# A transformer block and a routed block: the first projection's pages move to the normed input, the last nineteen of them in high and low halves

## The chip, the core and the metric

The kernel runs on one core of one Trainium2 chip. The metric is the device time of one execution in microseconds (us). Five engines take part: TensorE (PE in the rows, its weight loads PEld), VectorE (DVE), ScalarE (ACT), GpSimd (POOL), and SyncE (SP), which only issues DMAs here.

## What is computed

The reference is a mixing block on 256 tokens of width 1024, a feed-forward block, and a second block with product-key experts. What matters here is its beginning:

```python
h = rms_norm(x, norm1_g[l])
proj = h @ w_in[l]
p_rwkv, p_sb, q_mem, gate_logits = jnp.split(proj, cut, axis=-1)

def rms_norm(x, g, eps=NORM_EPS):
    xf = x.astype(jnp.float32)
    y = xf * lax.rsqrt(jnp.mean(xf * xf, axis=-1, keepdims=True) + eps)
    return (y * g.astype(jnp.float32)).astype(x.dtype)

def token_shift(p, mu):
    prev = jnp.pad(p, ((0, 0), (1, 0), (0, 0)))[:, :-1]
    return p + (prev - p) * mu
```

The first 1792 columns of `proj` (14 tiles of 128) go through `token_shift` and then into a recurrence whose triangular systems the kernel solves by repeated squaring on blocks of 32, 64 and 128 tokens. The next 12 tiles are the queries and keys of the stick-breaking attention and the queries of the memory attention.

## The kernel before

Features lie on the 128 partitions, tokens on the free axis. A weight page is 128 x 1024 float32 (512 KB): the weights of one output tile of 128 features, read as eight 128 x 128 blocks. SyncE streams all pages in one order through a ring of four slots; a slot is loaded again once TensorE has counted its page in `page_done`. Four PSUM banks (0 to 3) take the output tiles of the pages in turn, so tile n waits until tile n-4 is out of its bank (`bank_free`, by the table `OWNER`). Banks 4 to 7 serve the small products in between.

Stage `in_a` has 26 pages, numbered 0 to 25. `a_page` multiplies page by page in float32, eight matmuls of 256 columns each, with `xg`, the input times its gain but not yet divided by its root mean square; that division is made on the way out. `evict(b, shift)` on VectorE waits for page b, multiplies the bank by the reciprocal root (L1634) and, for the first 14 pages, makes the token shift with three more operations (L1638 to L1640). `A_ORDER` gives the tile of each page: two tiles of low-rank inputs, the keys, the receptances, the values, then the 12 tiles without shift.

Between the pages stand the small products of the recurrence, written out by hand in one order for each engine, with counting semaphores: `b_pe`, `b_act` and `b_dve` carry named steps. The ones that matter here: `kk_sq` (squares of the keys, DVE L1684), `kk_sum` (their sums, PE L603, after page 8), the square root on ACT (L1146), the reciprocal on DVE (L1710, `kk_inv`), the spread of it on PE (L608, after page 11), the cumulated log decay on DVE (scans L1696 and L1703, L1713 and L1714, `cum_ready`), its exponentials on ACT (L1148 to L1150), the products with them on DVE up to `scaled` (L1741), and then the first near products on PE (L636), before and after page 18. Pages 19 to 25 alternate with products of 32 x 32 blocks (L516) and of pairs (L542). `pairs(j)` on PE waits until DVE has read `pairs(j-1)` (`pairs_read`).

The full normed input `hn` is made by `norm_apply(0, ...)` on DVE behind `evict(19)`. A later stage, `gate0` and `gate1`, already works in halves: `high(page)` on ACT rounds a page to float32r (L1101), `low(n)` on POOL subtracts this from the page (L2303), TensorE makes three one-pass products (high x high, high x low, low x high) in place of one float32 product, and the rounded input `hn_hi` and its rest `hn_lo_early` are made once (ACT L1173, DVE L1791). POOL does nothing else before that but two trees of three additions each (L2334), which sum the squares of the input and of the memory; the second one waits for `kk_sq`. `norm_apply(1, ...)`, the normed memory, follows `evict(23)`, and a memset of `DT` stands behind `kk_sq` (L1685).

## Time and profile before

| | |
|---|---|
| Median of 3 runs | 1410.83 us (1409.07 to 1412.17) |
| The profiled execution's own time | 1410.49 us |
| Its span in the trace | 1408.7 us |
| PE busy | 1277.8 us, 91% of the span |
| DVE, ACT, POOL busy | 835.1, 626.1, 583.8 us |
| Granted TensorE clock, mean | 0.993 of full |

A busy time says how long an engine had an instruction running, not that it was needed for the end; the profiled time is 1.8 us over the span, and 0.34 us under the median of the runs. The stage `in_a` fills the span from about 8.6 us to 133.7 us.

### The profile page before, as it was taken

The page shows a single profiled execution, that of the slowest core. Times are in us where ns is not written, and L with a number is a line of the kernel's source. Part 1 is how long each engine was busy: PE and PEld are TensorE (multiplying, and loading weights), DVE is VectorE, ACT ScalarE, POOL GpSimd, SP SyncE. Part 2 cuts the span into 40 slices and gives each one's busy share as a digit, 9 for nine tenths or more (in the row PEclk, how much of TensorE's full clock was granted, in tenths as well). Part 3 has the DMA queues.
Part 4 walks back from the last instruction along what each step waited for, and adds up shares of the span by engine and source line. Part 5 has one row for each costly group of instructions (what it writes and reads, how often), then busy time and mean ns, then how long its engine had stood idle before and what let it go on. Part 6 is the DMA issues. An engine that isn't in the chain of part 4 may idle for free.

```text
span 1408.7 us, 22241 instructions
## 1 busy us (share of the span) xinstructions
PE 1277.8 (91%) x8716; PEld 902.6 (64%) x8716; DVE 835.1 (59%) x1898; ACT 626.1 (44%) x1451; POOL 583.8 (41%) x390
## 2 busy tenths in 40 slices
PE   7999999999999999999999999999777778877786
PEld 6888897989999999987897544444222223222222
DVE  3865201454557873477347766667776666677754
ACT  4210232656566664553454544444443444444433
POOL 1100022515878889740043444444434443443341
PEclk9999999999999999999999999999999999999999
DMA  6332322324645555443369999999999999999995
GB/s 241 120 117 83 106 91 74 120 92 149 194 158 188 181 186 191 164 135 99 135 235 390 396 421 421 422 421 421 422 422 421 421 421 422 421 422 422 421 422 230
DMA packets 67652, 381.06 MB, mean 271 GB/s; under 512 B 7520, under 2 KB 7648, under 8 KB 34528
## 3 DMA queue, kind: packets, MB, share of 16 engines
q0 software_dynamic: 36864, 268.45, 46.0%
q1 hardware_dynamic: 29808, 107.49, 23.0%
q10 hardware_dynamic: 880, 3.76, 0.8%
q8 instruction: 65, 1.06, 0.3%
q14 instruction: 35, 0.29, 0.1%
HBM read 378.63 MB, written 1.05 MB: 270 GB/s over the span
## 4 chain that ended last, share of the span: by engine, by line
PE 61%; DMA 26%; DVE 5%; ACT 5%; issue 2%; POOL 1%; DVEq 0%; POOLq 0%; ACTq 0%
DMA arena_block<-in_experts,arena_block 26%; PE bank L429 25%; PE bank L1041 10%; PE bank L465 4%; PE bank L981 3%; PE bank L483 3%; DVE arena_block L2247 2%; PE bank L427 2%; PE bank L447 2%; PE bank L853 1%; PE bank L516 1%; ACT arena_block L1535 1%; PE bank L542 1%; ACT arena_block L1533 1%; POOL w_lo L2305 1%
## 5 line engine op out<-in xcount | busy, mean ns | idle before, releaser
L1041 PE MATMUL bank<-arena_block 128*128 128x512 f32 x1024 | 493.7, 617 | 101.6 <-ACT arena_block L1535 101.5
L1041 PEld LDWEIGHTS bank<-arena_block 128*128 128x128 f32 x1024 | 182.3, 192 | 400.9 <-ACT arena_block L1535 247.7
L2247 DVE SCALAR_TENSOR_TENSOR arena_block<-arena_block 128x1024 f32<-128x1024 f32 x256 | 313.5, 1226 | 196.8 <-DMA arena_block<-in_experts,arena_block 196.2
L2323 POOL DMA_INDIRECT arena_block<-in_experts,arena_block x256 | 271.6, 1061 | 378.8 <-PE bank L1041 349.9
L2305 POOL TENSOR_TENSOR w_lo<-ring,w_hi 128x1024 fp32r<-128x1024 f32 x108 | 262.2, 2447 | 184.4 <-ACT w_hi L1101 183.9
L1529 ACT ACTIVATE arena_block<-arena_block 128x1 f32<-128x1 f32 x256 | 51.8, 202 | 322.9 <-DVE arena_block L2247 322.6
L1101 ACT ACTIVATE w_hi<-ring 128x1024 fp32r<-128x1024 f32 x116 | 122.0, 1054 | 60.4 <-PE bank L465 28.8
L429 PE MATMUL bank<-x_hi,w_hi 128*128 128x256 f32 x384 | 109.3, 285 | 1.6 <-POOL w_lo L2305 1.5
L429 PE MATMUL bank<-arena_mix,ring 128*128 128x256 f32 x480 | 109.1, 384 | 0.0
L429 PE MATMUL bank<-x_lo,w_hi 128*128 128x256 f32 x384 | 108.7, 283 | 0.0
L429 PE MATMUL bank<-x_hi,w_lo 128*128 128x256 f32 x384 | 108.7, 283 | 0.0
L1535 ACT ACTIVATE arena_block<-const,arena_block 128x128 f32<-128x128 f32 x256 | 102.7, 401 | 8.3
L429 PEld LDWEIGHTS bank<-arena_mix,ring 128*128 128x128 f32 x480 | 90.4, 191 | 16.0 <-issue 4.1
L2303 POOL TENSOR_TENSOR ring_lo<-ring,early_hi 128x1024 fp32r<-128x1024 f32 x8 | 19.9, 2488 | 171.4 <-ACT early_hi L1101 171.4
L1533 ACT ACTIVATE arena_block<-arena_block 128x1 f32<-128x1 f32 x256 | 75.4, 295 | 9.3
L429 PEld LDWEIGHTS bank<-x_hi,w_hi 128*128 128x128 f32 x384 | 73.7, 192 | 2.0 <-POOL w_lo L2305 2.0
L429 PEld LDWEIGHTS bank<-x_lo,w_hi 128*128 128x128 f32 x384 | 73.7, 192 | 0.1
L429 PEld LDWEIGHTS bank<-x_hi,w_lo 128*128 128x128 f32 x384 | 73.7, 192 | 0.0
L429 PE MATMUL bank<-h_norm,ring 128*128 128x256 f32 x224 | 51.6, 383 | 0.0
L465 PE MATMUL bank<-ff_hi,w_hi 128*128 128x256 f32 x176 | 49.8, 283 | 0.0
L465 PE MATMUL bank<-ff_lo,w_hi 128*128 128x256 f32 x176 | 49.8, 283 | 0.0
L465 PE MATMUL bank<-ff_hi,w_lo 128*128 128x256 f32 x176 | 49.8, 283 | 0.0
(512 smaller groups left out, 2245.1 us busy)
## 6 DMA issues: line engine op xcount, KB each, us to landing
ring<-in_pages SPq DMA_DIRECT2D x189, 512.0 KB, 3.9
late<-in_pages SPq DMA_DIRECT2D x11, 512.0 KB, 6.0
arena_block<-in_experts,arena_block POOLq DMA_INDIRECT x256, 15.3
x_res<-in_xT SPq DMA_DIRECT2D x2, 512.0 KB, 6.0
arena_mix<-in_memT ACTq DMA_DIRECT2D x1, 1024.0 KB, 10.7
arena_block<-in_subkT ACTq DMA_DIRECT2D x1, 1024.0 KB, 4.9
out_tok<-arena_block SPq DMA_DIRECT2D x4, 256.0 KB, 4.7
const<-in_const ACTq DMA_DIRECT2D x1, 974.5 KB, 6.8
```

The costliest lines, as they stand in the source:

```text
L429: last = mm(out[:, 0:T], w, y, **flags)
L465: last = mm(out[:, 0:T], w[:, at * P:(at + 1) * P], y[:, k, :], start=k == 0 and n_ == 0, stop=k == FT - 1 and n_ == 2)
L483: last = mm(bank_of(stage, 2 * b + t)[:, 0:T], w[:, t * 512 + k * P:t * 512 + (k + 1) * P], y[:, k, :], start=k == 0 and n_ == 0, stop=k = ...
L981: last = mm(bank[4 + b % 2][:, 0:T], w[:, k * P:(k + 1) * P], hn[:, k, :], start=k == 0, stop=k == KT - 1)
L1041: last = mm(bank[2 * tt + j][:, :], diag[:, slot, :], uv[slot][:, D + j * 512:D + (j + 1) * 512], start=False, stop=stop)
L1101: A_(w, ring[:, page % SLOTS, :], ACT.Copy).then_inc(S("hi_ready"), 1)
L1529: A_(e_gelu[:, s:s + 1], e_act[:, s:s + 1], ACT.Gelu).then_inc(S("gelu_ready"), 1)
L1533: A_(e_act[:, s:s + 1], e_gelu[:, s:s + 1], ACT.Copy, scale=gate_p[:, tt, m:m + 1]).then_inc(S("weight_ready"), 1)
L1535: A_(diag[:, s, :], ident, ACT.Copy, scale=e_act[:, s:s + 1]).then_inc(S("diag_ready"), 1)
L2247: stt(uv[s][:, 0:D], uv[s][:, 0:D], 1.0, htok[:, tt, :], ALU.mult, ALU.mult, accum_out=e_act[:, s:s + 1])\
L2305: nc.gpsimd.tensor_tensor(w_lo[:, slot, :], ring[:, slot, :], w_hi[:, slot, :].bitcast(F32), ALU.subtract)\
L2323: nc.gpsimd.indirect_dma_start(out=uv[slot], out_offset=None, in_=A["experts"], in_offset=bass.IndirectOffsetOnAxis(ap=eidx[:, tt, m:m + 1 ...
```

## The change

Pages 0 to 4 stay as they are. Pages 5 and 6 are multiplied, still in float32, with `hn`, and pages 7 to 25 in high and low halves of page and input. For this `hn` is made right behind `evict(1)`; ACT rounds it (`hn_hi_first`), DVE makes the rest (`hn_lo_early`), ACT rounds the nineteen pages and POOL makes their low halves in place of the ring's slot. Since `hn` is divided by the root already, the outputs are not scaled any more. For pages 5 to 13 ACT writes (1 - mu) times the bank into `proj` (`a_part`) and DVE adds mu times the bank shifted by one token (`shift`). Pages 14 to 25 are copied out by ACT (`a_copy`); DVE has nothing to do with them. The second tree of POOL stands behind the second low half, the memset of `DT` and the normed memory behind `near_cross(3)`.

```diff
-SPLIT = EARLY + [p for p in range(SPLIT0, N_PAGES) if p not in WHOLE]
+SHIFTED, ROWED, FIRST_SPLIT = 14, 5, 7
+FIRSTS = list(range(PAGE0["in_a"] + FIRST_SPLIT, PAGE0["in_a"] + N_IN_A))
+IN_PLACE = FIRSTS + EARLY
+SPLIT = IN_PLACE + [p for p in range(SPLIT0, N_PAGES) if p not in WHOLE]
+OWNER[SHIFTED:N_IN_A] = [("in_a_copy", i) for i in range(N_IN_A - SHIFTED)]
...
         def a_page(first, n=1):
-            linear("in_a", xg, part=(first, n))
+            for b in range(first, first + n):
+                if b < ROWED:
+                    linear("in_a", xg, part=(b, 1))
+                    continue
+                if b == ROWED:
+                    pe.wait_ge(S("norm_out"), 1)
+                if b == FIRST_SPLIT:
+                    pe.wait_ge(S("hn_low_early"), 1)
+                if b < FIRST_SPLIT:
+                    linear("in_a", hn, part=(b, 1))
+                else:
+                    linear("in_a", hn_hi_first, hn_lo_early, part=(b, 1))
...
+        def a_part(b):
+            act.wait_ge(S("page_done"), PAGE0["in_a"] + b + 1)
+            i = A_ORDER[b]
+            A_(proj[:, i, :], bank_of("in_a", b)[:, 0:T], ACT.Identity, scale=mu_rest[:, i:i + 1]).then_inc(S("in_a_part"), 1)
+        def a_copy(b):
+            act.wait_ge(S("page_done"), PAGE0["in_a"] + b + 1)
+            A_(proj[:, A_ORDER[b], :], bank_of("in_a", b)[:, 0:T], ACT.Copy).then_inc(S("in_a_copy"), 1)
+        def a_high(b):
+            high(PAGE0["in_a"] + b)
...
+        act.wait_ge(S("norm_out"), 1)
+        A_(hn_hi_first, hn, ACT.Copy).then_inc(S("hn_first"), 1)
+        a_high(7)
...
         act.wait_ge(S("b_dve"), B_DVE["kk_mean"])
         A_(row[0:8, :], row[0:8, :], ACT.Sqrt).then_inc(S("b_act"), 1)
+        a_part(9)
+        a_high(12)
+        a_part(10)
         act.wait_ge(S("b_dve"), B_DVE["cum_ready"])
         A_(tmp1, cc, ACT.Exp).then_inc(S("b_act"), 1)
+        a_high(13)
+        a_part(11)
...
+        def shift(b):
+            i = A_ORDER[b]
+            dve.wait_ge(S("in_a_part"), b - ROWED + 1)
+            stt(proj[:, i, 1:T], bank_of("in_a", b)[:, 0:T - 1], V("mu", i), proj[:, i, 1:T], ALU.mult, ALU.add).then_inc(S("in_a_out"), 1)
...
-        evict(0, True)
-        evict(1, True).then_inc(S("b_dve"), 1)
-        for b in range(2, 6):
-            last = evict(b, True)
+        evict(0)
+        evict(1).then_inc(S("b_dve"), 1)
+        norm_apply(0, x, "norm1_g", hn)
+        for b in range(2, ROWED):
+            last = evict(b)
         step(last)
+        dve.wait_ge(S("page_done"), PAGE0["in_a"] + ROWED)
+        dve.wait_ge(S("hn_first"), 1)
+        tt_(hn_lo_early, hn, hn_hi_first.bitcast(F32), ALU.subtract).then_inc(S("hn_low_early"), 1)
+        shift(5)
...
         tt_(tmp2, kk, kk, ALU.mult).then_inc(S("b_dve"), 1)
-        v.memset(DT, 0.0)
         dve.wait_ge(S("b_act"), B_ACT["lora_taken"])
...
         near_cross(3)
+        dve.wait_ge(S("in_a_copy"), N_IN_A - SHIFTED)
+        v.memset(DT, 0.0)
+        norm_apply(1, mem_raw, "mem_g", memn)
         pairs_read(6)
...
-        for i in range(2):
+        def square_tree(i):
...
+        square_tree(0)
         for n in range(len(SPLIT)):
             low(n)
+            if n == 1:
+                square_tree(1)
```

On POOL, from the start of the program: arena_mix rows are the trees, ring_lo rows the low halves. Before, both trees stand ahead of the low halves, the first of which belongs to a gate page:

```order
L2334 TENSOR_TENSOR arena_mix<-arena_mix 128x1024
L2334 TENSOR_TENSOR arena_mix<-arena_mix 128x512
L2334 TENSOR_TENSOR arena_mix<-arena_mix 128x256
L2334 TENSOR_TENSOR arena_mix<-arena_mix 128x1024
L2334 TENSOR_TENSOR arena_mix<-arena_mix 128x512
L2334 TENSOR_TENSOR arena_mix<-arena_mix 128x256
L2303 TENSOR_TENSOR ring_lo<-ring,early_hi 128x1024 x2
```

and with the change:

```order
L2420 TENSOR_TENSOR arena_mix<-arena_mix 128x256
L2390 TENSOR_TENSOR ring_lo<-ring,first_hi 128x1024
L2390 TENSOR_TENSOR ring_lo<-ring,w_hi 128x1024
L2420 TENSOR_TENSOR arena_mix<-arena_mix 128x1024
L2420 TENSOR_TENSOR arena_mix<-arena_mix 128x512
L2420 TENSOR_TENSOR arena_mix<-arena_mix 128x256
L2390 TENSOR_TENSOR ring_lo<-ring,w_hi 128x1024
L2390 TENSOR_TENSOR ring_lo<-ring,first_hi 128x1024 x2
```

The first of these rows closes the first tree; two low halves (pages 7 and 8) now stand between the trees, and seventeen more follow the second.

On ACT, from the copies of the output gate (two rows of 128x512) to the first exponential. Before:

```order
L1143 ACTIVATE arena_mix<-bank 128x512 [waits b_pe]
L1144 ACTIVATE arena_mix<-bank 128x512
L1146 ACT_TABLE_LOAD
L1146 ACTIVATE arena_mix<-arena_mix 8x256 [waits b_dve]
L1148 ACT_TABLE_LOAD
L1148 ACTIVATE arena_mix<-arena_mix 128x1024 [waits b_dve]
```

and with the change (L1149 is `a_part`, L1128 is `a_high`):

```order
L1149 ACTIVATE arena_mix<-bank,arena_mix 128x256 [waits page_done]
L1128 ACTIVATE first_hi<-ring 128x1024 [waits page_done,page_in2]
L1149 ACTIVATE arena_mix<-bank,arena_mix 128x256 [waits page_done]
L1128 ACTIVATE first_hi<-ring 128x1024 [waits page_done,page_in3]
L1199 ACT_TABLE_LOAD
L1199 ACTIVATE arena_mix<-arena_mix 8x256 [waits b_dve]
L1149 ACTIVATE arena_mix<-bank,arena_mix 128x256 [waits page_done]
L1128 ACTIVATE w_hi<-ring 128x1024 [waits page_done,page_in0]
L1149 ACTIVATE arena_mix<-bank,arena_mix 128x256 [waits page_done]
L1204 ACT_TABLE_LOAD
L1204 ACTIVATE arena_mix<-arena_mix 128x1024 [waits b_dve]
L1128 ACTIVATE w_hi<-ring 128x1024 [waits page_done,page_in1]
```

Behind the square root (L1199) now stand the parts of pages 9 and 10 and the high half of page 12, behind the exponential (L1204) the high half of page 13.

## Rows read from the trace of the kernel before

**Rows 1.** Windows: length, PE, PEld, DVE, ACT, POOL busy, clock, DMA share, GB/s.

```profile
29.00:32.00 3.00, 2.95 (x16) 2.55 (x16) 0.49 (x2) 0.00 (x0) 0.00 (x0) 0.60 0.21 82
32.00:160.00 128.00, 127.46 (x2253) 107.54 (x2252) 77.01 (x163) 18.59 (x33) 6.31 (x3) 1.00 0.33 105
```

**Rows 2.** Chain that ended last, 0 to 200 us: start, us, what.

```profile
50.25 10.56 PE bank L429 x48
...
60.82 1.99 PE bank L608 x8
...
86.75 1.22 PE bank L636 x78
87.97 3.65 PE bank L429 x16
...
93.87 3.46 PE bank L429 x16
...
116.97 0.52 issue
```

**Rows 3.** Timeline, PE: start, us, instruction; a gate page and its successor.

```profile
213.30 0.39 PE L429 MATMUL bank<-hn_hi,w_hi 128*128 128x256 f32 x1
...
216.28 0.89 PE L565 MATMUL bank<-arena_mix 128*128 128x64 f32 x7
```

**Rows 4.** Timeline, PE, the one idle stretch near the page stage.

```profile
29.05 0.45 PE L592 MATMUL bank<-arena_mix 64*128 64x256 f32 x1 [2.23 <-ACT arena_mix L1135]
```

**Rows 5.** Timeline, POOL, 40 to 47 us: the second tree.

```profile
40.46 4.32 POOL L2334 TENSOR_TENSOR arena_mix<-arena_mix 128x1024 f32<-128x1024 f32 x1 [23.36 <-DVE arena_mix L1684]
...
44.85 2.07 POOL L2334 TENSOR_TENSOR arena_mix<-arena_mix 128x512 f32<-128x512 f32 x2
```

**Rows 6.** Timeline, DVE, same stretch, and source view of L1688.

```profile
40.66 1.76 DVE L1685 MEMSET arena_mix<- 128x2048 f32 x1 [0.38 <-issue]
42.34 2.58 DVE L1688 TENSOR_SCALAR arena_mix<-arena_mix,vec 128x256 f32<-128x256 f32 x2
...
44.85 2.22 DVE L1688 TENSOR_SCALAR arena_mix<-arena_mix,vec 128x256 f32<-128x256 f32 x2
...
L1688 DVE TENSOR_SCALAR arena_mix<-arena_mix,vec x4: 231/1152/2439, 42.3 to 46.2; 128x256 f32<-128x256 f32 x4
```

**Rows 7.** Timeline, DVE and POOL, where two-input operations meet a low half.

```profile
200.39 2.38 POOL L2303 TENSOR_TENSOR ring_lo<-ring,w_hi 128x1024 fp32r<-128x1024 f32 x1 [3.01 <-ACT w_hi L1101]
...
202.26 1.59 DVE L1798 TENSOR_TENSOR arena_mix<-arena_mix 128x1024 f32<-128x1024 f32 x1
...
270.08 1.22 DVE L1880 TENSOR_TENSOR arena_mix<-arena_mix 128x1024 f32<-128x1024 f32 x1
...
270.18 3.35 POOL L2303 TENSOR_TENSOR ring_lo<-ring,early_hi 128x1024 fp32r<-128x1024 f32 x1 [2.29 <-ACT early_hi L1101]
```

**Rows 8.** Groups by line, DVE, 32 to 84 us: busy us, mean ns.

```profile
L1640 DVE SCALAR_TENSOR_TENSOR arena_mix<-arena_mix,vec 128x256 f32<-128x256 f32 x9 | 4.4, 485 | 0.3
...
L1684 DVE TENSOR_TENSOR arena_mix<-arena_mix 128x1024 f32<-128x1024 f32 x1 | 1.2, 1225 | 0.0
...
L1682 DVE TENSOR_SCALAR arena_mix<-arena_mix,vec 128x256 f32<-128x256 f32 x4 | 1.1, 350 | 0.0
```

**Rows 9.** Timeline, DVE: reciprocal, normed input, its low half.

```profile
59.04 1.73 DVE L1710 RECIPROCAL arena_mix<-arena_mix 8x256 f32<-8x256 f32 x1
...
97.70 3.24 DVE L1611 SCALAR_TENSOR_TENSOR h_norm<-x_res,vec,arena_mix 128x256 f32<-128x256 f32 x8
...
173.80 2.29 DVE L1791 TENSOR_TENSOR hn_lo_early<-h_norm,hn_hi 128x2048 fp32r<-128x2048 f32 x1
```

**Rows 10.** ACT: timeline of one copy; groups by line, 0 to 300 us.

```profile
166.22 1.90 ACT L1173 ACTIVATE hn_hi<-h_norm 128x2048 fp32r<-128x2048 f32 x1
...
L1101 ACT ACTIVATE w_hi<-ring 128x1024 fp32r<-128x1024 f32 x8 | 8.4, 1049 | 0.4 <-DMA ring<-in_pages 0.4
```

**Rows 11.** DMA issues, 30 to 140 us: KB each, median us to landing.

```profile
ring<-in_pages SPq DMA_DIRECT2D x22, 512.0 KB, 3.6
```

More of the change, by code:

```diff
@@ L220, in build @@
     row, row2, col = at(W0 + 19736, T), at(W0 + 18200, T), at(W0 + 19992, 32)
+    mu_rest = at(W0 + 20024, SHIFTED)
     ITEMS = 16
@@ L254, in build @@
     early_hi = [typed(start, f"early_hi{i}", 4).rearrange("p a b -> p (a b)") for i, start in enumerate((19968, W0 + 8192))]
+    first_hi = [typed(start, f"first_hi{i}", 4).rearrange("p a b -> p (a b)") for i, start in enumerate((13824, 14848))]
+    hn_hi_first = typed(9728, "hn_hi_first", KT)
     y_hi, y_lo = typed(18944, "y_hi", 8), typed(11776, "y_lo", 8)
@@ L267, in build, with high_room @@
     x_hi, x_lo = (sb(n, [P, KT, T], F32R) for n in ("x_hi", "x_lo"))
+    first_hi = [w_hi[:, 0, :], w_hi[:, 1, :]] + first_hi
+    def high_room(page):
+        if page in FIRSTS:
+            return first_hi[page % SLOTS]
+        if page in EARLY:
+            return early_hi[(page - EARLY[0]) % SLOTS]
+        return w_hi[:, page % SLOTS, :]
     ff_space = [nc.sbuf_tensor(n, [P, FT, T], F32R) for n in ("ff_hi", "ff_lo")]
@@ L363, in _ @@
         for page in range(SLOTS, LATE0 - 1):
-            if page - SLOTS in NTH and page - SLOTS not in EARLY:
+            if page - SLOTS in NTH and page - SLOTS not in IN_PLACE:
                 sp.wait_ge(S("lo_ready"), NTH[page - SLOTS])
@@ L405, in products @@
                 return [(ring[:, slot, :], hn if page in WHOLE else hi)]
-            if page in EARLY:
-                high, low = early_hi[(page - EARLY[0]) % SLOTS], ring_lo[:, slot, :]
+            if page in IN_PLACE:
+                high, low = high_room(page), ring_lo[:, slot, :]
                 return [(high, hi), (high, lo), (low, hi)]
@@ L1169, in _ @@
             A_(PPn, two(bank[6][:, :], NEAR), ACT.Copy).then_inc(S("b_act"), 1)
+            if lv == 0:
+                a_copy(19)
+                a_high(22)
+                a_high(23)
+                a_copy(20)
+                a_high(24)
+                a_copy(21)
+            if lv == 1:
+                a_copy(22)
+                a_high(25)
+                a_copy(23)
+                a_copy(24)
+            if lv == 2:
+                a_copy(25)
         take("sbv", flat(sbv), part=(3, 1))
@@ L1690, in _ @@
         stt(raw_k, tmp1, 1.0, raw_k, ALU.add, ALU.mult)
-        evict(6, True)
+        shift(6)
         step(ts(logw, logw, DECAY_SCALE, None, ALU.mult))
@@ L1703, in _ @@
                 v.tensor_tensor_scan(cc[:, ft, r], ones[:, 0:1].broadcast_to([P, P]), logw[:, ft, r], 0.0, ALU.mult, ALU.add)
-        evict(8, True)
-        step(evict(9, True))
+        shift(8)
+        shift(9)
+        dve.wait_ge(S("in_a_out"), 10)
         for ft in range(4):
```

83 lines of the change are left out of this document (44 added, 39 removed).

## The prediction

> **What bounds the stretch.** I read the windows first. From 32 to 160 us TensorE is busy 127.46 of 128 us at full clock, VectorE 77, ScalarE 19, GpSimd 6 [rows 1]: the reader is to see that this stretch is as long as its matmuls, and that GpSimd is all but free. The chain says the same in detail: float32 pages at 3.46 us each (three in 10.56) or 3.65 behind a small product, with the small products between them and one 0.52 us pause [rows 2]. A saved matmul would therefore be saved time, if the other engines keep up. How near they are the chain doesn't tell; one row does: the reciprocal for the keys ends at 59.04 + 1.73 = 60.77 [rows 9], and TensorE uses it at 60.82 [rows 2]. That edge has no slack.
>
> **What TensorE saves.** A page in halves already runs in the gate stage: it starts at 213.30, and the next product starts at 216.28, so 2.98 us for 24 one-pass matmuls [rows 3], against 3.65. Inside a run of pages I put the same 0.19 between first and later pages as before, 2.87 at the least. Pages 7 and 8 save 1.1, 9 to 11 1.8, 12 0.7, 13 to 15 1.6, 16 and 17 0.5 each, 18 to 25 0.5 to 0.67 each, 5.2: 11.4 us in all. Pages 5 and 6 stay float32: nothing.
>
> **What the others do for it.** Per page ScalarE rounds (1.05) [rows 10], GpSimd subtracts (2.38) [rows 7], behind a load that lands in 3.6 [rows 11]. With the product that is 3.6 + 1.05 + 2.38 + 2.98 = 10.0 us for a slot, against four pages, 11.9: supply alone fits. The normed input moves ahead: 3.24 on VectorE [rows 9], from 25.4, where the shift of page 1 ends, to 28.6, its rounding 1.90 [rows 10] to 30.8 on ScalarE, its rest 2.29 [rows 9] on VectorE. Page 5 can't start before 32.3 anyway, since it stands behind the product that waits for ScalarE at 29.05 [rows 4]: free. The shift loses VectorE time: four operations an output, of which one of 0.49 [rows 8] stays. VectorE had been idle 51 of 128 us [rows 1], so by itself this gives nothing; ScalarE's copies lie beside matmuls.
>
> **The price: VectorE and GpSimd exclude each other.** In the second tree the first addition takes 4.32 us, where a subtraction of the same width takes 2.38 [rows 5, 7]; it had to let the memset of 1.76 through. Behind it four operations of 256 columns on VectorE, 0.35 each elsewhere [rows 8], take 2.58 + 2.22: the source view has one at 0.23 and one at 2.44 us [rows 6], which is GpSimd's addition waited out. GpSimd's next two (2.07 together) [rows 5] were let in between the third and the fourth. So as long as GpSimd has work, they take turns, one instruction each. Operations with two inputs in SBUF are caught too: one of 1.23 [rows 8] took 1.59, started while a low half had 0.5 to go, and a low half of 2.38 took 3.35 behind one [rows 7]. A shift that reads PSUM and one SBUF input is not seen waiting. The Trainium skill ("SBUF — State Buffer", section "Who interferes with whom") calls the shared port pair an exclusive lock for the whole instruction and counts every VectorE operation with two SBUF inputs; here the traced rows agree for additions, and no row of before has a scan beside GpSimd. If the eight scans wait as that rule says, and a low half falls among them, the sum below is one turn, 2.2, longer, and the gain gone.
>
> From page 7's low half (32.0) to `scaled` the lock is asked for by 11 low halves and the tree, 11 x 2.38 + 2.4 + 2.07 = 30.6, and by VectorE: 2.3 for the rest of the input, seven operations of full width at 1.23 (8.6), two groups of four of 256 columns and one input (2.8), three groups of four with two (5), the scaling of the decays and the scans, which I estimate from the 256-column rows at 0.7 and 2.8. That is 22, together 53, less some 0.15 of overlap a turn: about 50 of the 55 us between 32 and 86.75, where TensorE starts the near products now [rows 2]. It fits only if nobody ever waits for something else.
>
> **Laid out in turn** (each from the durations above). Low halves 7 and 8 end at 34.4 and 38.9, the tree at 43.4, low half 9 at 45.8; between them VectorE gets one operation a turn, so the squares of the keys are ready at 47.0 instead of 40.3 (where they release the second tree now [rows 5]): still ahead of TensorE, which ends page 8 at 47.4. The next group alternates with low halves 10 and 11; the shift of page 6 comes at 54.1, and page 10 waits for its bank, 1.9 us. The sums' minimum is at 56.9, and here ScalarE's order bites: the high half of page 12 stands behind the square root, is done at 58.9, and its low half takes the lock at 59.0, just ahead of the four two-input operations in front of the reciprocal. They end at 62.9, the reciprocal at 64.6: TensorE, through with page 11 at 60.0, waits 4.6 us. Then the cumulated decay is ready at 67.3, the high half of page 13 behind its exponential at 69.3, its low half at 71.8; pages 13 to 17 and the small products fill TensorE to 89.2. On VectorE the products with the exponentials take turns with low halves 16, 17 and 18, and `scaled` comes at 89.6. So the near products start 2.85 us later than at 86.75, all that pages 7 to 17 saved being eaten.
>
> Behind that GpSimd has slack (a page each 5 to 6 us with the small products), VectorE little to do: pages 18 to 25 save their 5.2, and the pause of 0.52 goes. Then the moved memset and normed memory: they stand ahead of `pairs_read(6)`, and TensorE needs that read after one more page. The memset can start 1.0 after the square product, and 1.76 + 3.24 + 1.35 for the read end 1.25 us after TensorE wants it (0.0 before). The memset behind `kk_sq` is gone from there, counted above. From here on everything shifts as a block: the later stages read nothing else of the change, and the rest of the input, 2.29 on VectorE at 173.8 [rows 9], had nobody waiting.
>
> **Sum:** 2.85 - 5.2 - 0.5 + 1.25 = -1.6 us. The profiled execution (1410.49, 0.34 under the median of 1410.83) would go to 1408.9, the median to **1409.2**.
>
> **The rivals.**
> *TensorE stays the bound (0.20).* If two-input operations mostly slip past GpSimd (the 1.59 row waited only 0.36 of the 0.5 left), or low halves fall into VectorE's idle moments, the 11.4 come through, less 1.25 at the memset and about 1.1 for page 13's low half: -9, **1402**. For it: VectorE has 51 idle us [rows 1] and loses 39 operations, 27 at pages 5 to 13 and 12 at the rest; against it the turns in rows 5 and 6, where the same tree and the same group of four meet again.
> *The clock falls in the new waits (0.12), slower.* After 2.23 us without a matmul [rows 4] the granted clock was 0.60 over 29 to 32 us [rows 1], which is mostly the lower level, 1.2 GHz: the eight small matmuls there take 3.3 us, until page 5 starts, where the eight at 60.82 take 1.99 [rows 2]; with the page behind them I put 2.0 on such a wait. My layout has three new waits, 1.9, 4.6 and 1.25 us. If each costs that much and the chain through VectorE doesn't hide it, +6.0 - 1.6 = +4.4, **1415.2**. It decides from the point where a wait passes about 2 us; against it, the two first lie where VectorE is the later one anyway.
> *The halves don't arrive (0.08).* ScalarE serves copies and rounding in one fixed order; if its waits on VectorE hold back pages 12 to 18 by a further microsecond or two, the gain is used up: 1409.5 to 1413, no change.
> *My layout* has 0.60. Its own range is one turn (2.2) either way and some more where a group slips through whole: 1405.5 to 1412.
>
> **Numbers.** A measurement can tell about 0.2%, 2.8 us, from no change. Faster by more: all of the first rival and a third of the layout, 0.41; slower: the clock rival and a tail of the layout, 0.15; the rest, 0.44, within. The range takes in the first rival and the layout with its unknowns: 1402 to 1413.5.
>
> **What would show it.** Right: VectorE operations of 0.35 to 1.23 us stretched to 2.4 to 3.6 between 37 and 90 us, the reciprocal ending near 64.6, TensorE idle before the spread, near products at about 89.6, page 25 done about 2.9 us earlier than before, and a short idle before `pairs(7)`. A step each is wrong if the stretched operations are absent, if TensorE is still busy over 98% from 41 to 90 us, or if a window there shows the clock well below 1.00. The forecast is wrong if the near products start before 86 us.

## The result, and the profile after

| | before | after |
|---|---|---|
| median of the runs, us | 1410.47 | 1417.69 |
| lowest to highest, us | 1408.85 to 1412.46 | 1415.55 to 1421.16 |
| profiled execution, us (span) | 1410.49 (1408.7) | 1417.12 (1415.3) |
| mean granted clock | 0.993 | 0.988 |

The change makes the kernel slower: ratio 1.0056, interval 1.0048 to 1.0065, some 7.2 us of the medians (8 runs each). The forecast was 1409.2.

The page of the kernel after, its first lines and its instruction queue:

```profile
span 1415.3 us, 22587 instructions
...
PE 1273.0 (90%) x8868; PEld 905.1 (64%) x8868; DVE 838.6 (59%) x1860; ACT 654.3 (46%) x1492; POOL 636.3 (45%) x409
...
q8 instruction: 66, 1.08, 0.3%
```

TensorE has less to do and still ends later. The two windows that stand in [rows 1], now of the kernel after:

```profile
29.00:32.00 3.00, 2.48 (x16) 2.14 (x16) 2.86 (x10) 3.00 (x3) 0.00 (x0) 0.75 0.34 130
32.00:160.00 128.00, 116.67 (x2264) 105.20 (x2262) 81.27 (x121) 43.49 (x72) 54.04 (x22) 0.97 0.30 101
```

Between 32 and 160 us TensorE was idle 0.54 us before, and is idle 11.33 now; GpSimd went from 6.31 to 54.04. VectorE issues 42 instructions fewer and is busy longer, since many of the operations left last longer. Its timeline up to the reciprocal (start, us, instruction):

```profile
37.88 6.45 DVE L1782 TENSOR_SCALAR arena_mix<-arena_mix,vec 128x256 f32<-128x256 f32 x4
44.37 3.38 DVE L1784 TENSOR_TENSOR arena_mix<-arena_mix 128x1024 f32<-128x1024 f32 x1
47.67 5.38 DVE L1787 TENSOR_SCALAR arena_mix<-arena_mix,vec 128x256 f32<-128x256 f32 x4
...
57.00 0.40 DVE L1798 TENSOR_SCALAR arena_mix<-bank 8x256 f32<-8x256 f32 x1
...
59.48 3.60 DVE L1807 SCALAR_TENSOR_TENSOR arena_mix<-arena_mix,vec 128x256 f32<-128x256 f32 x4
63.00 1.73 DVE L1810 RECIPROCAL arena_mix<-arena_mix 8x256 f32<-8x256 f32 x1
```

Four operations of 256 columns take 6.45, 5.38 and 3.60 us; the last four take 1.67 where GpSimd leaves the port alone (first experiment). GpSimd's timeline beside them, the low halves of pages 8 to 12 and the second tree:

```profile
36.50 3.12 POOL L2390 TENSOR_TENSOR ring_lo<-ring,w_hi 128x1024 fp32r<-128x1024 f32 x1 [1.70 <-ACT w_hi L1128]
39.58 4.60 POOL L2420 TENSOR_TENSOR arena_mix<-arena_mix 128x1024 f32<-128x1024 f32 x3
44.26 2.40 POOL L2390 TENSOR_TENSOR ring_lo<-ring,w_hi 128x1024 fp32r<-128x1024 f32 x1
46.62 5.75 POOL L2390 TENSOR_TENSOR ring_lo<-ring,first_hi 128x1024 fp32r<-128x1024 f32 x2
59.23 2.37 POOL L2390 TENSOR_TENSOR ring_lo<-ring,w_hi 128x1024 fp32r<-128x1024 f32 x1 [6.86 <-ACT w_hi L1128]
```

TensorE's timeline: every wait and pause between 50 and 180 us (in brackets how long it was idle and what ended it), and the near products for their place. A row marked "issue" is a pause in which TensorE waits for nothing that the profile shows.

```profile
54.84 0.35 PE L445 MATMUL bank<-hn_hi_first,first_hi 128*128 128x256 f32 x1 [2.08 <-DVE arena_mix L1734]
...
64.78 1.64 PE L636 MATMUL bank<-arena_mix,const 8*128 8x256 f32 x3 [3.96 <-DVE arena_mix L1810]
...
90.34 1.29 PE L664 MATMUL bank<-arena_mix 64*32 64x32 f32 x128
...
95.68 1.23 PE L664 MATMUL bank<-arena_mix 64*32 64x32 f32 x121 [0.80 <-issue]
...
99.96 0.27 PE L669 MATMUL bank<-const,arena_mix 128*128 128x128 f32 x1 [2.14 <-issue]
...
105.10 0.41 PE L544 MATMUL bank<-arena_mix 32*32 32x32 f32 x26 [0.90 <-issue]
...
144.53 0.26 PE L544 MATMUL bank<-arena_mix 32*32 32x32 f32 x7 [0.99 <-issue]
145.15 1.14 PE L570 MATMUL bank<-arena_mix 64*128 64x256 f32 x8 [0.36 <-DVE arena_mix L1760]
...
165.44 0.48 PE L445 MATMUL bank<-arena_mix,ring 128*128 128x256 f32 x1 [0.34 <-issue]
165.85 1.27 PE L544 MATMUL bank<-arena_mix 32*32 32x32 f32 x127
168.90 0.21 PE L544 MATMUL bank<-arena_mix 32*32 32x32 f32 x1 [1.78 <-issue]
169.04 5.41 PE L445 MATMUL bank<-arena_mix,ring 128*128 128x256 f32 x16
```

The first two are the waits on VectorE that the forecast had. The six "issue" pauses it did not have: TensorE stops **in the middle** of a product, sometimes one instruction short of its end. They sum to 6.95 us, where before has the one of 0.52 [rows 2].

Where the 6.6 us of the two spans arise, from the start of the same instruction in both timelines:

| reached by TensorE | before | after | difference | what it grew by |
|---|---|---|---|---|
| first near product | 86.68 | 90.34 | +3.66 | +3.66 |
| end of page 25 | 133.71 | 136.34 | +2.63 | -1.03 |
| `pairs(7)` | 140.91 | 145.15 | +4.24 | +1.61 |
| end of page `mk(1)` | 165.91 | 174.45 | +8.54 | +4.30 |
| end of the span | 1408.7 | 1415.3 | +6.6 | -1.9 |

The last stretch took 1240.4 to 1244.9 us in the fourteen traces of this study, so its -1.9 is within what it varies by.

The +3.66 has a part that the forecast left out. After the wait of 3.96 us TensorE's clock is low, and from there to the near products TensorE is never idle; VectorE, which the forecast had as the later one, stands idle three times meanwhile for outputs of TensorE that ScalarE copies (2.82 us for page 13's):

```profile
65.00:73.00 8.00, 8.00 (x34) 6.73 (x35) 4.38 (x7) 5.25 (x7) 3.61 (x2) 0.60 0.00 0
```

```profile
76.77 0.48 DVE L1734 SCALAR_TENSOR_TENSOR arena_mix<-bank,vec,arena_mix 128x255 f32<-128x255 f32 x1 [2.82 <-ACT arena_mix L1149]
```

TensorE ends page 17 at 90.30 and VectorE the scaled decays at 90.28: both bound the near products. The spread and page 12 took 3.77 and 4.44 us instead of 1.99 and 3.13, 3.1 lost. My estimate of what that cost the near products is 1.2 us: page 13 started at 73.00, and at full clock it would have waited for its low half, which was done at 71.79.

### The profile page after: what moved, and what is told of

Read it like the earlier page. It is cut to its first block, busy times and chain, and to the rows that moved or that the text cites. A ratio compares the mean times of both kernels' runs of the same rounds, so it can differ in the third digit from the quotient of the medians.

```text
span 1415.3 us, 22587 instructions
## 1 busy us (share of the span) xinstructions
PE 1273.0 (90%) x8868; PEld 905.1 (64%) x8868; DVE 838.6 (59%) x1860; ACT 654.3 (46%) x1492; POOL 636.3 (45%) x409
## 3 DMA queue, kind: packets, MB, share of 16 engines
q8 instruction: 66, 1.08, 0.3%
## 4 chain that ended last, share of the span: by engine, by line
PE 57%; DMA 26%; DVE 8%; ACT 5%; issue 2%; POOL 1%; DVEq 0%; POOLq 0%; ACTq 0%
DMA arena_block<-in_experts,arena_block 25%; PE bank L445 22%; PE bank L1069 10%; PE bank L481 4%; PE bank L1009 3%; PE bank L499 3%; DVE arena_block L2335 2%; PE bank L443 2%; PE bank L463 2%; PE bank L881 1%; PE bank L544 1%; ACT arena_block L1622 1%; ACT arena_block L1620 1%; POOL w_lo L2392 1%; PE bank L570 1%
## 5 line engine op out<-in xcount | busy, mean ns | idle before, releaser
L2410 POOL DMA_INDIRECT arena_block<-in_experts,arena_block x256 | 276.2, 1079 | 374.0 <-PE bank L1069 342.8
L1128 ACT ACTIVATE w_hi<-ring 128x1024 fp32r<-128x1024 f32 x126 | 132.6, 1054 | 63.7 <-PE bank L481 28.5
L2390 POOL TENSOR_TENSOR ring_lo<-ring,w_hi 128x1024 fp32r<-128x1024 f32 x18 | 45.3, 2518 | 65.0 <-ACT w_hi L1128 64.9
L445 PE MATMUL bank<-h_norm,ring 128*128 128x256 f32 x256 | 59.5, 387 | 0.0
L445 PEld LDWEIGHTS bank<-h_norm,ring 128*128 128x128 f32 x256 | 48.1, 192 | 8.7 <-issue 2.4
```

Of the source, the lines that this page charges most:

```text
L445: last = mm(out[:, 0:T], w, y, **flags)
L1128: A_(high_room(page), ring[:, page % SLOTS, :], ACT.Copy).then_inc(S("hi_ready"), 1)
L2390: nc.gpsimd.tensor_tensor(ring_lo[:, slot, :], ring[:, slot, :], high_room(SPLIT[n]).bitcast(F32), ALU.subtract).then_inc(S("lo_ready"), 1)
L2410: nc.gpsimd.indirect_dma_start(out=uv[slot], out_offset=None, in_=A["experts"], in_offset=bass.IndirectOffsetOnAxis(ap=eidx[:, tt, m:m + 1 ...
```

## The experiments

**1. GpSimd's low halves cut to one column (narrow17).** It tells the port from ScalarE's order. Pages 7 to 17 multiply the rounded page a third time in place of its low part.

```diff
-                high, low = high_room(page), ring_lo[:, slot, :]
+                high, low = high_room(page), high_room(page) if page in FIRSTS and page < 18 else ring_lo[:, slot, :]
...
+            if SPLIT[n] in FIRSTS and SPLIT[n] < 18:
+                r = slice(0, 1)
+                nc.gpsimd.tensor_tensor(ring_lo[:, slot, r], ring[:, slot, r], high_room(SPLIT[n]).bitcast(F32)[:, r], ALU.subtract).then_inc(S("lo_ready"), 1)
+                return
```

> The changed kernel, with GpSimd's subtraction for pages 7 to 17 cut to one column, and the third product of these pages reading the rounded page again, so that the matmuls stay the same in number and size (the output of these pages loses the low part). Turns at the port as the cause of the late near products: VectorE's operations of 256 columns between 37 and 90 us go back from 0.85 to 1.6 us each to 0.25 to 0.35, the reciprocal ends near 57 instead of 64.7, TensorE's wait of 4.0 us for it is gone, and the near products start at 81 to 82.5 us instead of 90.3. The rival, ScalarE's fixed order (copies and rounding before what VectorE waits for): the reciprocal and the near products move by under 2 us. In total the first theory says 5 to 9 us less than the changed kernel: less than the 8 to 9 at the near products if pauses of TensorE without a releaser grow where its work becomes denser, which a theory of too slow an instruction supply says; if the pauses of 6.9 us are of the clock after the 4.0 us wait, they should be under 2 us here.

Measured: 1411.26 us (10 runs, 1404.5 to 1415.2), 6.4 us less than the changed kernel and no less than the kernel before (1.0002, interval 0.9987 to 1.0018); the execution that was profiled took 1414.99, 3.7 over that median. The reciprocal ends at 56.65, and the near products start at 81.83, 8.5 earlier. Of its timelines, VectorE and TensorE:

```profile
53.33 1.67 DVE L1807 SCALAR_TENSOR_TENSOR arena_mix<-arena_mix,vec 128x256 f32<-128x256 f32 x4
54.92 1.73 DVE L1810 RECIPROCAL arena_mix<-arena_mix 8x256 f32<-8x256 f32 x1
```

```profile
81.83 1.29 PE L664 MATMUL bank<-arena_mix 64*32 64x32 f32 x128
...
91.37 0.37 PE L669 MATMUL bank<-const,arena_mix 128*128 128x128 f32 x1 [2.69 <-issue]
...
116.95 0.70 PE L570 MATMUL bank<-arena_mix 64*128 64x256 f32 x4 [2.95 <-issue]
```

GpSimd's work at the port, with the waits that it made and the low clock behind the longer of them, is what held up the near products; ScalarE's order stayed as it was. But with neither of the waits of 2.1 and 4.0 us the "issue" pauses are longer, 8.0 us in all, so they are no after-effect of those waits. They took away all of the head start: at the end of page `mk(1)` it is 170.72 against 165.91 before.

**2. Halves for pages 18 to 25 alone (split18).**

```diff
-SHIFTED, ROWED, FIRST_SPLIT = 14, 5, 7
+SHIFTED, ROWED, FIRST_SPLIT = 14, 5, 18
...
-            high(PAGE0["in_a"] + b)
+            if b >= FIRST_SPLIT:
+                high(PAGE0["in_a"] + b)
...
-            if n == 1:
-                square_tree(1)
+        pool.wait_ge(S("b_dve"), B_DVE["kk_sq"])
+        square_tree(1)
```

> The changed kernel with halves for pages 18 to 25 alone; pages 7 to 17 are float32 pages that read the normed input, and the second tree stands behind the squares of the keys again. Turns at the port as what ate the gain: near products start at 85.5 to 87 us (86.75 before). Then pages 18 to 25 save 5.2 and the read of pairs(7) costs 1.5. Pauses without a releaser: if they are TensorE's instructions coming too slowly in pages of 24 short matmuls, 2 to 4 us of them stay between 88 and 175 us and the total is 1407 to 1410; if they came from the clock or from the turns before them, under 1 us stays and the total is 1405 to 1407, below both kernels by more than 4 us.

Measured: 1408.41 us (10 runs), against before 0.9986, interval 0.9976 to 0.9996: 1.8 us less. Near products at 85.89, `pairs(7)` waits 1.56 for VectorE, and three pauses of 0.59, 1.48 and 0.93 remain. So the pauses need neither the waits nor the turns of pages 7 to 17. They don't need the denser pages either: the kernel before has one of 0.52, and two of 1.55 together when it is displaced (next experiment).

**3. and 4. The instruction stream displaced (after_pad32, before_pad32).** The work stays as it is; small matmuls move all that follows to another place in the stream.

```diff
         a_page(3, 2)
+        for _ in range(32):
+            mm(bank[7][0:32, 0:32], x[:, 0, 0:32], x[:, 0, 0:32], start=True, stop=True)
```

> The changed kernel with 32 small float32 matmuls (32x32) added in TensorE's idle time ahead of the product for the projections of lower rank, at 29 us; nothing reads them. They displace everything behind them in TensorE's instruction stream, and leave its work alone. If the pauses without a releaser (0.80 at 94.9, 2.14 at 97.8, 0.90 at 104.2, 0.99 at 143.5, 1.78 at 167.1 us) depend on where in the instruction stream a dense piece falls, they come at other instructions or with other lengths (by 0.5 us or more each); their sum stays 4 to 8. If they belong to the work at that place (contention, a transfer, the clock), the same instructions have the same pauses to 0.2 us. Total within 3 us of the changed kernel by either, near products at 90.3.

> The kernel before with the same 32 small matmuls at the same place. If pauses depend on the place in the instruction stream, the 0.52 us one near 97 to 98 us changes its length or place, and the sum of pauses between 80 and 175 us can be anything from 0 to 3 us, with the total changed by as much. If it belongs to the work there, it stays at 0.5 us and the total is within 1 us of the kernel before.

Measured: 1415.46 us (5 runs) and 1409.96 (10 runs; 0.9997, interval 0.9987 to 1.0006). In the changed kernel so displaced the near products start at 91.43 us, a little later, yet the stretch behind them is nearly free of pauses. The waits of TensorE between 80 and 180 us, by line (sum, times, longest), for that kernel:

```profile
PE bank L570 <- DVE arena_mix L1763: 1.6, 1, 1.6
PE bank L713 <- ACT arena_mix L1272: 1.1, 1, 1.1
PE bank L570 <- issue: 0.8, 1, 0.8
PE bank L544 <- issue: 0.2, 1, 0.2
```

6.95 us of pauses became 1.1. In before the one of 0.52 went (it stood at 116.97 us, not at 97 to 98 as the expectation says), and two others of 0.36 and 1.19 came, at other instructions. The pauses belong to the place in the instruction stream. My expectation of 4 to 8 us for the sum was wrong: it can nearly vanish. The median fell by only 2.2, the profiled execution, the fastest of the five, by 4.1. The near products are later although the reciprocal ends 0.3 earlier: page 12 took 5.49 us there, at the low clock, instead of 4.44.

The pauses are not the whole of the loss. The two displaced kernels compared with each other, with 1.1 and 1.55 us of pauses, still differ by 2.9 us in their profiled executions (spans 1411.2 and 1408.3) and by 5.5 in their medians, the changed one slower: its near products start 5.8 later, and pages 18 to 25 win back 3.3.

**What they wait for.** The profile has an instruction queue, q8, of 66 packets and 1.08 MB [page above], 16 KB each. TensorE's 2 x 8868 records (a record is a row of the trace, one for each matmul and one for each weight load) over 66 packets are 269 to a packet, and a kernel with 512 records more (experiment 5) has 68 packets: they carry TensorE's instructions, 256 each. The view of the queues over a tenth of a microsecond tells when a packet starts and, by its share of 16 engines' time, how long it takes. For the kernel after, 97.5 to 97.6 us:

```profile
q8 instruction: 1, 0.02, 58.2%
```

That is 0.582 x 16 x 0.1 = 0.93 us. Narrower windows put its start at 97.60, so it ends at 98.53; TensorE, paused since 97.82, goes on at 99.96. All pauses of that trace, and the one of before:

| kernel | pause | packet starts | takes | TensorE goes on | behind the packet's end |
|---|---|---|---|---|---|
| after | 0.80 | 93.34 | 0.88 | 95.68 | 1.46 |
| after | 2.14 | 97.60 | 0.93 | 99.96 | 1.43 |
| after | 0.90 | 102.47 | 1.33 | 105.10 | 1.30 |
| after | 0.99 | 141.92 | 1.30 | 144.53 | 1.31 |
| after | 0.34 | 162.99 | 0.89 | 165.44 | 1.56 |
| after | 1.78 | 166.48 | 1.01 | 168.90 | 1.41 |
| before | 0.52 | 115.16 | 0.96 | 117.49 | 1.37 |

In all 14 traces of this study there are 52 such pauses of 0.25 us or more, all between 76 and 182 us, and every one ends 1.2 to 1.6 us behind the end of an instruction packet. In none of the traces does a packet start less than 3.28 us after the one before it. The test by exception came with the last kernel below: one packet there took 2.33 us beside a page load instead of about 1 (it starts at 93.89; the row of 93.8 to 93.9 us), and TensorE paused until 97.53, again 1.3 behind its end.

```profile
q8 instruction: 1, 0.02, 145.4%
```

Where the pauses stand is more exact still. Counted from the start of the trace, with TensorE's few semaphore instructions, they stand in the kernel after behind 1217, 1473, 1729, 4033, 5058 and 5314 instructions, and in before behind 2498: each is 193 or 194 over a multiple of 256, and so are all 52 in the 14 traces. Two windows of the kernel after, from the start to just before the first and the second pause's end, show the distance without the 22 semaphore instructions, 597 + 598 and 725 + 726 records, 256 apart:

```profile
0.00:95.67 95.67, 80.55 (x597) 70.78 (x598) 65.93 (x95) 44.95 (x72) 46.76 (x24) 0.95 0.46 161
0.00:99.95 99.95, 82.69 (x725) 72.75 (x726) 68.82 (x103) 44.95 (x72) 46.76 (x24) 0.95 0.46 159
```

So TensorE pauses only where a new packet of 256 begins, and not at each. A near product is 256 records (128 matmuls, 128 weight loads) in 1.29 us, and a page in halves 48 in 3.1 where the float32 page has 32 in 3.7. One round with its page and its small products, in the windows of before and of after:

```profile
99.53:105.47 5.94, 5.94 (x155) 4.83 (x153) 3.77 (x10) 0.00 (x0) 0.00 (x0) 1.00 0.29 101
```

```profile
111.84:117.19 5.35, 5.35 (x163) 4.80 (x161) 2.30 (x6) 1.45 (x2) 2.69 (x2) 1.00 0.30 93
```

That is 308 records in 5.94 us before, 52 in a us, and 324 in 5.35 now, 61. That packets are used up faster behind the dense products now, so that more of them come late, is my reading of it; how many TensorE has in store no view shows. A fixed rate is not the whole of it: the two packets ahead of the pause of 0.90 each start 4.3 and 4.9 us after the one before, well over the shortest distance of 3.28. The Trainium skill ("Runtime: NRT & Kernel Launch", section "Instruction fetch mechanics") says that the sequencer refills its store through a DMA queue of its own in blocks of 16 KiB, 256 instructions, at a cost "mostly hidden". The blocks are those seen here; hidden they are not in this stretch.

**5. Displaced by whole packets (after_pad128).** The same edit with 128 in place of 32.

> The changed kernel with 128 of the small matmuls (32x32, nothing reads them) in TensorE's idle time at 29 us. They are 256 records of TensorE (a weight load and a matmul each), which at 64 B each is just one of the 16 KB packets of the instruction queue. Supply theory: all 18 pauses without a releaser in the six traces so far ended 2.3 to 2.8 us after an instruction packet had started, and packets never follow one another in under 3.4 us; a shift by a whole packet changes nothing, so the pauses come back at the same instructions as in the changed kernel (0.80 in the second near product, 2.14 at its last transpose, 0.90, 0.99 and 1.78 in the products of 32x32), each to within 0.4 us, where the shift by 64 records left 1.1 of 6.9 us. Total within 1.5 us of the changed kernel plus whatever the 128 matmuls run past their gap (under 1 us). Rival (the pauses have to do with the clock or with what the small matmuls do for it): the sum of pauses is near that of the run with 32 matmuls, 1 to 2 us, and the total is 1415 or less.

Measured: 1421.64 us (4 runs). TensorE's rows for the small matmuls and two pauses:

```profile
28.10 8.29 PE L618 MATMUL bank<-x_res 128*32 128x32 f32 x256
...
100.31 1.23 PE L667 MATMUL bank<-arena_mix 64*32 64x32 f32 x121 [0.25 <-issue]
...
105.14 0.27 PE L672 MATMUL bank<-const,arena_mix 128*128 128x128 f32 x1 [2.69 <-issue]
```

The first row corrects my count: a float32 product leaves two matmul records (x256 for 128) and two weight loads, so this is 512 records, two packets of 256, and the 32 of experiment 3 were 128 records, half a packet. The test stands: displaced by whole packets, the pauses are back at the same instructions, the second near product behind its seventh matmul record as before (x121 to go), the last transpose (2.69), the 32x32 products (1.18, 1.32, 1.78), the page ahead of the last (0.61), with one new of 1.33; 9.2 us in all, in an execution of 1425.83 us, the slowest of the four. Of the five I named, three lie within the 0.4 us allowed and two are 0.55 off. That half a packet removes most of them and two packets bring them back is what a supply in packets says. The clock doesn't: both displaced kernels had it at 1.00 from 29 to 32 us. (The 3.4 us between packets of the expectation is a little high: 3.30 to 3.34 stand in four of those six traces.) The matmuls themselves took 8.29 us, not the 3 or so I had put, so they delay everything by 5.2.

**6. The rounding of page 12 ahead of the square root (high12_early).**

```diff
-        act.wait_ge(S("b_dve"), B_DVE["kk_mean"])
-        A_(row[0:8, :], row[0:8, :], ACT.Sqrt).then_inc(S("b_act"), 1)
         a_part(9)
         a_high(12)
+        act.wait_ge(S("b_dve"), B_DVE["kk_mean"])
+        A_(row[0:8, :], row[0:8, :], ACT.Sqrt).then_inc(S("b_act"), 1)
```

> The changed kernel with ScalarE's rounding of page 12 (and the copy of page 9) moved ahead of the square root of the key norms. Port theory: the low half of page 12 then takes the port while VectorE waits for ScalarE's root or one group earlier, so the four products at 59.5 us (3.60 us) take 1.4 to 2.5, the reciprocal ends 1 to 2.2 us earlier than 64.7, and TensorE's wait of 4.0 us becomes 1.8 to 3; near products up to 1.5 us earlier. If VectorE's group is slow by itself or the port only slides the turn to another group, nothing changes (reciprocal within 0.5 us). Total between -2 and 0 us against the changed kernel plus or minus 2 for other pauses.

Measured: 1416.73 us (4 runs). The four products are free, and another operation has paid, VectorE's timeline:

```profile
54.72 2.61 DVE L1791 TENSOR_SCALAR arena_mix<-arena_mix 128x1024 f32<-128x1024 f32 x1
...
61.50 1.67 DVE L1807 SCALAR_TENSOR_TENSOR arena_mix<-arena_mix,vec 128x256 f32<-128x256 f32 x4
63.09 1.73 DVE L1810 RECIPROCAL arena_mix<-arena_mix 8x256 f32<-8x256 f32 x1
```

The products went from 3.60 to 1.67, but start 2.0 later, since the scaling ahead of the scans now takes 2.61 instead of 0.68. The reciprocal is 0.1 later than in the changed kernel, and TensorE waits 2.09, 1.20 and 2.54 us where it waited 2.08 and 3.96. Of my two outcomes it is the second: here the turn slid to where GpSimd asked instead, at 54.38, and cost the same there, 1.93 us.

**7. The memset moved (split18b).** As 2, and:

```diff
         near_cross(3)
+        pairs_read(6)
         dve.wait_ge(S("in_a_copy"), N_IN_A - SHIFTED)
-        v.memset(DT, 0.0)
-        norm_apply(1, mem_raw, "mem_g", memn)
-        pairs_read(6)
         tt_(sq_of["sbq"], sbq, sbq, ALU.mult)
         pairs_read(7)
+        v.memset(DT, 0.0)
         near_add(2)
+        norm_apply(1, mem_raw, "mem_g", memn)
```

> The version with halves for pages 18 to 25 alone, and the memset and the normed memory put behind the reads that TensorE waits for (read of pairs(6) first, then the squares, the read of pairs(7), the memset; the normed memory behind near_add(2)). The wait of 1.56 us in pairs(7) goes; nothing new waits. Total 1.5 us less than the version without that move (1408.4), 1406 to 1408, if the pauses for instructions stay about 3 us. If the wait was covered by another, it stays at 1408.4 (within 0.5).

Measured: 1408.19 us (10 runs; 0.9987, interval 0.9977 to 0.9996). The wait of 1.56 is gone from the profile, and the median is only 0.2 lower, with a spread of the runs of 4 to 5 us: the total doesn't settle it. The profiled executions show what came in its place. The near products start 1.26 later (87.15 against 85.89), since the clock was 0.73 from 29 to 32 us here and 1.00 in experiment 2. The pauses are 3.36 us against 3.0. And behind the one of 1.75 the clock fell:

```profile
132.73 2.04 PE L570 MATMUL bank<-arena_mix 64*128 64x256 f32 x8
134.71 4.55 PE L443 MATMUL bank<-ring,h_norm 128*128 128x128 f32 x32
```

In experiment 2 these two took 1.13 and 3.84 us, so a pause of 1.75 cost 1.6 more than its length.

**8. Halves from page 14 on (split14b).** As 7 with `FIRST_SPLIT` 14.

> The same with halves from page 14 on, twelve pages. In the kernel before, the scaled decays were ready at 81.7 us and TensorE started the near products at 86.7: 5 us of slack for VectorE. Port theory: the low halves of pages 14 to 18 put four to five turns (about 1.2 to 2.2 us each) into VectorE's work between 65 and 85 us; scaled comes at 84 to 88 us, TensorE at 84.6 if alone, so pages 14 to 17 save 0 to 2 us over halves from page 18. Total 1404.5 to 1408. If VectorE's turns are dearer than that, near products start later than 87 us and it is worse than halves from page 18.

Measured: 1408.82 us (10 runs; 0.9987, interval 0.9977 to 0.9996). Near products at 84.55, 2.1 earlier than before, just behind the scaled decays (84.49 against 81.69 before): the slack of VectorE is spent exactly. The pauses are 1.62, 1.36, 0.92 and 0.28, and the total is 0.8 above the range that I expected.

**9. to 12. The same with 16, 32 and 8 small matmuls (s14_plus16, s14_plus32, s14_plus16_again, s14_plus8).** By the count of experiment 5 they are 64, 128 and 32 records, not half of that as the expectations say. A version with 48 was planned and has no measurement.

> Halves from page 14 on, memset moved, and 16 of the small matmuls (32 records) in the idle time at 29 us, where they cost nothing. In the version without them TensorE paused 1.62, 1.36, 0.92 and 0.28 us for instructions. Supply theory: other pauses, their sum anywhere from 1 to 5 us (4.2 without the matmuls), each ending 2.3 to 2.8 us after an instruction packet started; the total follows the sum, 1406 to 1410.

> The same with 32 small matmuls (64 records), which fill the idle time just so. Supply theory: as with 16, another sum of pauses from 1 to 5 us, total 1406 to 1410; in the changed kernel this shift took 5.9 us of pauses away. Near products at 84.5 us in all of these, since nothing on the way to them changes.

> The fastest version so far (halves from page 14 on, memset moved, 16 small matmuls in the idle time) once more, with more rounds. It had 1407.49 us over 5 runs, from 1403.5 to 1408.8. If the place of the instruction blocks sets the pauses, this profile has them at the same four instructions (0.35, 2.52, 0.64 and 1.54 us, each within 0.6), with near products at 83.6 us; the median lies between 1405.5 and 1408.5, below the kernel before by 0.15 to 0.35%.

> The same with 8 small matmuls (16 records, half the shift). Supply theory: as the shift is small, the pauses sit near those with 16 or with none, their sum 3 to 5.5 us, each 2.3 to 3.0 us behind the start of an instruction packet; total 1406 to 1409.

| kernel | median us (runs) | against before, interval | near products at | pauses |
|---|---|---|---|---|
| split14b | 1408.82 (10) | 0.9987 (0.9977 to 0.9996) | 84.55 | 4.2 |
| s14_plus16 | 1407.49 (5) | 0.9965 (0.9947 to 0.9983) | 82.6 | 5.05 |
| s14_plus16_again | 1405.37 (10) | 0.9966 (0.9955 to 0.9976) | 83.06 | 3.25 |
| s14_plus32 | 1410.42 (10) | 1.0005 (0.9988 to 1.0021) | 83.2 | 5.2 |
| s14_plus8 | 1403.27 (5) | 0.9940 (0.9927 to 0.9953) | 83.23 | 2.05 |

The near products start 1.3 to 1.9 us earlier with small matmuls than without, not at 84.5 as expected, since page 5 does (30.9 to 31.5 us against 32.4; last section). Totals and pauses left the expected ranges on both sides: s14_plus32 has 5.2 us of pauses and 1410.42 where up to 5 and 1410 were expected, s14_plus8 2.05 and 1403.27 where 3 to 5.5 and 1406 to 1409 were, and the second run of s14_plus16 lies 0.1 below its range. The theory says where pauses can stand, not how long they are.

The one kernel profiled twice shows how far a profile of pauses repeats: 0.35, 2.52, 0.64, 1.54 in the first, and in the second 0.31, 2.52, none, 0.42, each at the same instruction. The place is fixed, the length isn't.

With 8 the waits of TensorE between 80 and 180 us are:

```profile
PE bank L445 <- issue: 1.5, 1, 1.5
PE bank L713 <- ACT arena_mix L1273: 1.1, 1, 1.1
PE bank L544 <- issue: 0.5, 1, 0.5
```

This version, twelve pages in halves, the memset behind the reads and 8 small matmuls, is the fastest of the study, 0.6% below the kernel before (5 runs) and 1% below the changed one. Part of that is the clock at 29 us (last section).

## Why the prediction was wrong

By its own steps:

- **The layout in turn** was right nearly row by row. Forecast against measured: squares of the keys ready 47.0, 47.75; page 10 waits 1.9, 2.08; the sums' minimum 56.9, 57.40; low half 12 takes the port 59.0, 59.23; the four products end 62.9, 63.08; reciprocal ends 64.6, 64.73; TensorE waits 4.6, 3.96; scaled 89.6, 90.28; near products 2.85 later, 3.66 later. Experiment 1 shows the cause by taking GpSimd off the port, experiment 6 that a turn can be moved and not lost. But the last two of these agree by some luck. The forecast had the clock at full speed and named a clock well below 1.00 between 41 and 90 us as a sign against it; the window of 65 to 73 us has 0.60. It had TensorE stand still for page 13's low half until 71.8; the low half did come at 71.79, but TensorE, slow, reached page 13 only at 73.00. These 1.2 us cover the missing 0.8.
- **"All that pages 7 to 17 saved being eaten"** held.
- **"Pages 18 to 25 save their 5.2, and the pause of 0.52 goes"** is the step that failed. It is -5.7 in the sum and measured -1.03. The pages did become shorter: a round takes 5.34 instead of 5.93 us. But three pauses, 0.80, 2.14 and 0.90, came with them, 3.84. In its own terms: the pages saved 4.36 instead of 5.2, the 0.52 went, and 3.84 that the sum put at nothing came in, 1.03 in all. The 0.52 in [rows 2] was read as a blemish that would go; it was the one trace in before of TensorE standing still at the start of an instruction packet, and the change feeds it 48 records a page where there were 32.
- **The memset and the normed memory**, +1.25, measured +1.61 in this trace, of which the wait is 0.36: a pause of 0.99 in the product ahead hid the rest. In experiment 2 the wait itself is 1.56. Right in kind, and near in size.
- **"From here on everything shifts as a block"** failed too, by +4.3 between `pairs(7)` and page `mk(1)`, a stage in which not one instruction of TensorE was changed. There are 2.12 us of pauses, at packet starts that lie at other instructions since everything behind the halves has moved in the stream, and a page that runs 5.41 instead of 3.72 us behind one of them: 1.7 of clock (0.69 of full from 169 to 174.5 us). The remaining 0.5 is not traced.
- Later stages gave back 1.9, for which I had nothing; the wait of 0.71 at 330 us of before is not there after. The rest is not traced, and the stretch varies by more than that from trace to trace.

The sum with what was measured: 3.66 - 1.03 + 1.61 + 4.30 - 1.9 = +6.6, against -1.6. Of the 8.2 us between them the two failed steps are 4.7 and 4.3, and the other terms -0.7 together. Without pauses the change would still not have gained what was forecast: experiments 3 and 4 have it 2.9 us slower with next to none.

**The rivals.** TensorE as the bound is out: near products at 90.3, where that case had them before 86. The clock rival named the right side, and its 1415.2 is the nearest figure of the list, but for a small part of the loss. It put 2.0 us on a wait; behind the wait of 3.96 it was 3.1, of which by my estimate 1.2 counted, since page 13's low half would have held up the rest. The text against it, that VectorE is the later one there anyway, is wrong: VectorE waited for TensorE's pages. Another 1.7 lay behind a pause that nobody had foreseen. No case in the list had a stall without a releaser, so the range (to 1413.5) could not reach 1417.7.

**Open.** What makes TensorE ask for a packet when it does, and why it pauses at one packet's start and not at the next, no view shows. How the pauses vary between executions is only seen through the totals (narrow17 from 1404.5 to 1415.2 with one and the same program). That denser pages make such pauses more frequent is argued from the counts of records, and from 1.1 to 9.2 us of them in the twelve traces with halves against 0.52 and 1.55 in the two without; after_pad32, with halves, had 1.1, and before_pad32, without, 1.55. In experiments 8 to 12 the totals go roughly with the sums of pauses, but s14_plus8 and s14_plus32 lie 7.2 us apart with 3.2 us between their pauses, so the pauses alone don't make the difference.

## What to carry to other kernels

A matmul that is split into cheaper ones costs instructions, and TensorE's instructions arrive in packets: where denser pages go between products that are dense already, read every "issue" row of the kernel before as a warning, and see whether such rows stand 256 records apart. A pause of 1.75 us or more can cost more than its length, since the clock may fall behind it. An engine with 40% idle time is no free place for work if it shares a port with the engine on the critical chain: here its low halves cost that engine turns, and moving one of them only moved the turn. When two engines arrive within a few hundredths of a us, both chains have to be read before the lateness is put down to one. Where such pauses exist, 32 to 96 records more ahead of them went with medians 2 to 7 us apart, so compare variants at more than one displacement before believing 0.3%.

## What was not expected of the hardware

- **TensorE pauses at the start of instruction packets**: 52 pauses of up to 2.95 us, all at 193 or 194 over a multiple of 256 instructions, each ending 1.2 to 1.6 us behind a packet's end, packets never closer than 3.28 us.
- **The clock can fall behind such a pause**: 1.00 turned into 0.69 behind the one of 1.78 (after) and 0.79 behind the one of 1.75 (split18b), while it stayed at 1.00 behind the one of 2.14 (after).
- **A few small matmuls in an idle gap keep the clock.** In before TensorE is idle 2.23 us ahead of the product at 29 us, and the window behind it has a clock of 0.60 [rows 1, 4]. With 32 small matmuls in the gap (before_pad32) the same window, and with 8 (s14_plus8):

```profile
29.00:32.00 3.00, 2.91 (x36) 2.47 (x34) 1.07 (x4) 0.81 (x3) 0.00 (x0) 1.00 0.35 138
```

```profile
29.00:32.00 3.00, 2.44 (x18) 2.11 (x19) 2.86 (x10) 2.62 (x4) 0.00 (x0) 1.00 0.32 128
```

  The clock stays at 2.4 GHz, and page 5 starts at 31.6 and 31.5 instead of 32.3; the near products of before_pad32 come 1.0 earlier. All seven traces with small matmuls in the gap show 1.00 in this window, and of the seven without six show 0.60 to 0.79; it isn't certain to fall without them, since split18 shows 1.00 there too. And the gain is small beside the pauses, which ate it in before_pad32.
- **The clock also fell without a wait.** In narrow17 TensorE was busy all of 60 to 70 us and page 12 still ran at half rate for part of it, 4.64 instead of 3.1 us, right behind the eight products of 8 rows. The window:

```profile
60.00:70.00 10.00, 10.00 (x70) 9.95 (x71) 3.80 (x9) 8.07 (x13) 0.57 (x3) 0.83 0.34 114
```

- **How dear the turns of short operations with one input in SBUF are**: that they wait, [rows 6] had shown; here eight `TENSOR_SCALAR` of 256 columns took 11.83 us (6.45 + 5.38), 0.35 each elsewhere [rows 8], and the second four of them 1.14 us in narrow17.
